# A three-mixer trunk on one core: sums of squares move from TensorE to VectorE, and the second layer's gates move into the first SSD turn

## The reference, cut to what matters

```
x = x + ab_mixer(rmsnorm(x))      # layer 0
x = x + c_mixer(rmsnorm(x))       # layer 1
y = rmsnorm(x)

_rms(x) = x * rsqrt(mean(x*x) + 1e-6)

# ab_mixer: 4 GLA heads and 4 mLSTM heads, each 512 wide
proj = h @ w_in_ab                # 2048 -> some 14,000 columns
o = recurrence(q, k, v, gates, state)            # per head
o = _rms(o) * norm_weight * silu(z)              # per head
y = o @ w_out_ab

# c_mixer: 64 SSD heads in 8 groups
z, xbc, dt = split(h @ w_in_c)
dt = softplus(dt + dt_bias); a = -exp(a_log)
xbc = silu(causal_conv4(xbc, conv_state))
y = ssd(xbc, dt, a, state)                       # decays exp(cumsum(dt*a))
y = _rms per group of (y * silu(z)); y = y @ w_out_c
```

## Time and profile before

| | |
|---|---|
| time, median of 3 runs | 2212.8 us (2210.91 to 2214.97) |
| the profiled execution: time, span | 2215.32 us, 2213.8 us |
| TensorE busy | 2108.5 us, 95% of the span |
| VectorE, ScalarE, GpSimd busy | 64%, 45%, 13% |
| DMA | 436.97 MB, mean 197 GB/s |
| granted TensorE clock, mean | 0.977 |

### The profile page before, as it was taken

The page is one execution under the profiler, slowest core; times in us unless marked ns, Lnnn a source line. Parts: engine busy times, 40 slices in busy tenths (PEclk is TensorE's granted clock), DMA queues, the critical chain, the costliest instruction groups (busy, mean ns, idle before and its releaser), DMA issues. The chain is left out here.

```text
span 2213.8 us, 41516 instructions
## 1 busy us (share of the span) xinstructions
PE 2108.5 (95%) x15171; PEld 1970.3 (89%) x15171; DVE 1416.6 (64%) x2602; ACT 1005.3 (45%) x1516; POOL 279.6 (13%) x423
## 2 busy tenths in 40 slices
PE   6999999999999999999999599999999999989997
PEld 4898989998989998998999599988989889879996
DVE  5553747566558475575644467887788788775544
ACT  3444444434433443343333346556466565564432
POOL 1010202010101011020100101121220211200000
PEclk8899999999999999999999799999999999999998
DMA  4484759485847568495965375665665765756851
GB/s 131 129 270 125 268 156 305 149 284 163 269 123 249 191 191 258 134 323 169 322 221 165 90 206 177 179 206 178 199 209 163 214 187 178 217 195 190 289 158 67
DMA packets 337191, 436.97 MB, mean 197 GB/s; under 512 B 17688, under 2 KB 296776, under 8 KB 335628
## 3 DMA queue, kind: packets, MB, share of 16 engines
q1 hardware_dynamic: 298476, 297.76, 44.3%
q0 software_dynamic: 38384, 137.67, 18.5%
q10 hardware_dynamic: 224, 0.05, 0.0%
HBM read 355.35 MB, written 80.06 MB: 197 GB/s over the span
## 5 line engine op out<-in xcount | busy, mean ns | idle before, releaser
L145 PE MATMUL bank<-xn_hi,w_hi 128*128 128x288 f32 x3584 | 1082.8, 302 | 26.3 <-issue 9.4
L146 PE MATMUL bank<-xn_lo,w_hi 128*128 128x288 f32 x3584 | 1063.6, 297 | 0.0
L147 PE MATMUL bank<-xn_hi,w_lo 128*128 128x288 f32 x3584 | 1061.1, 296 | 0.0
L132 DVE TENSOR_TENSOR w_lo<-w_raw,w_hi 128x1024 fp32r<-128x1024 f32 x512 | 624.5, 1224 | 628.3 <-ACT w_hi L126 618.8
L126 ACT ACTIVATE w_hi<-w_raw 128x1024 fp32r<-128x1024 f32 x512 | 541.2, 1060 | 947.8 <-PE bank L147 858.5
L145 PEld LDWEIGHTS bank<-xn_hi,w_hi 128*128 128x128 f32 x3584 | 679.2, 189 | 54.0 <-issue 39.5
L146 PEld LDWEIGHTS bank<-xn_lo,w_hi 128*128 128x128 f32 x3584 | 680.3, 190 | 5.6
L147 PEld LDWEIGHTS bank<-xn_hi,w_lo 128*128 128x128 f32 x3584 | 680.7, 190 | 0.0
L1258 DVE SCALAR_TENSOR_TENSOR state<-state,decay,bank 128x512 f32<-128x512 f32 x128 | 92.3, 742 | 0.0
L1865 POOL DMA_DIRECT2D out_ssm_s<-ssd_state x64 | 47.9, 756 | 307.7 <-DVE ssd_state L2293 244.3
L2132 ACT ACTIVATE ssd_state<-ssd_state,ssd_we 128x128 f32<-128x128 f32 x256 | 82.5, 414 | 0.0
(11 more groups left out here) (445 smaller groups left out, 2338.5 us busy)
## 6 DMA issues: line engine op xcount, KB each, us to landing
w_raw<-in_w_in_ab SPq DMA_DIRECT2D x224, 512.0 KB, 4.0
w_raw<-in_w_in_c SPq DMA_DIRECT2D x128, 512.0 KB, 4.1
w_raw<-in_w_out_ab SPq DMA_DIRECT2D x64, 512.0 KB, 4.8
w_raw<-in_w_out_c SPq DMA_DIRECT2D x64, 512.0 KB, 3.8
state<-in_state_gla POOLq DMA_DIRECT2D x32, 512.0 KB, 10.1
out_gla_s<-state POOLq DMA_DIRECT2D x32, 512.0 KB, 4.2
state<-in_state_mlstm_c POOLq DMA_DIRECT2D x32, 512.0 KB, 10.2
out_mc_s<-state POOLq DMA_DIRECT2D x32, 512.0 KB, 5.4
```

What stands on the lines that cost most here:

```text
L132: dve.tensor_tensor(core.w_lo[:, j], core.w_raw[:, j % RAW], core.w_hi[:, j].bitcast(F32), ALU.subtract).then_inc(ws["split"], 1)
L145: pe.matmul(banks[m][:, 0:T], core.w_hi[:, j, kk, col], hi[:, k], start=f, stop=False)
L146: pe.matmul(banks[m][:, 0:T], core.w_hi[:, j, kk, col], lo[:, k], start=False, stop=False)
L147: ins = pe.matmul(banks[m][:, 0:T], core.w_lo[:, j, kk, col], hi[:, k], start=False, stop=e)
```

## The change

1. **The three norms of the trunk** (setup and both rests): in place of sixteen ones products (`tensor_sum`, `t_sums`), VectorE copies the first squared tile to a buffer and adds fifteen (`vector_sum`), and TensorE runs one ones product over the sum (`tensor_total`). The rest's gate product goes to bank 4.
2. **AB heads:** VectorE adds four squared tiles in two instructions, and `t_rms` has one ones product.
3. **Gates:** the block `gates1` becomes the class `Gates1`, whose parts are placed in the first SSD turn: SP's loads ahead of the first group's, VectorE's parts at the turn's start and at steps 1, 2, 3, 4 and 6, ScalarE's at steps 0 and 2, TensorE's transposes at steps 3 and 5. POOL stores the tables (SP did) and waits for them and for the last copy before its loads of the group. The buffers lie over those of the mixer that are not yet used.

```diff
+    def vector_sum(self, dve, k, slot):
+        dve.wait_ge(self.squared, k + 1)
+        if isinstance(k, int) and k == 0:
+            dve.tensor_copy(self.tmp[:], self.sq[:, slot]).then_inc(self.sq_free, 1)
+        else:
+            dve.wait_ge(self.sq_free, k)
+            dve.tensor_tensor(self.tmp[:], self.tmp[:], self.sq[:, slot], ALU.add).then_inc(self.sq_free, 1)
+    def tensor_total(self, pe, bank):
+        pe.wait_ge(self.sq_free, KT)
+        pe.matmul(bank[:, 0:T], self.core.ones[:], self.tmp[:], start=True, stop=True).then_inc(self.total, 1)
...
                 dve.tensor_copy(xT[:, k], core.bank[k % 4][:, 0:T]).then_inc(norm.ready, 1)
+                if k >= 2:
+                    norm.vector_sum(dve, k - 2, (k - 2) % 4)
...
-                if k >= 3:
-                    norm.tensor_sum(pe, core.bank[4], k - 3)
-            for k in range(KT - 3, KT):
-                norm.tensor_sum(pe, core.bank[4], k)
+            norm.tensor_total(pe, core.bank[4])
...
-            pe.wait_ge(s["o_sq"], H + 1)
-            for f in range(4):
-                i = pe.matmul(B[6][:, 0:T], core.ones[:], sq[:, f], start=f == 0, stop=f == 3)
-            i.then_inc(s["rms"], 1)
+            pe.wait_ge(s["sq_sum"], H + 1)
+            pe.matmul(B[6][:, 0:T], core.ones[:], sq[:, 0], start=True, stop=True).then_inc(s["rms"], 1)
...
             if slot == 3:
+                dve.wait_ge(s["o_sq"], H + 1)
+                st.then_wait(dve.tensor_tensor(sq[:, 0:2], sq[:, 0:2], sq[:, 2:4], ALU.add))
+                dve.tensor_tensor(sq[:, 0], sq[:, 0], sq[:, 1], ALU.add).then_inc(s["sq_sum"], 1)
                 dve.wait_ge(s["rms"], H + 1)
...
             self.t_group(pe, pr * 2, 0)
-            self.t_sums(pe, (2, 3), pr * 4 - 2)
             self.t_group(pe, pr * 2 + 1, 1)
-            self.t_sums(pe, (0, 1), pr * 4)
-        self.t_sums(pe, (2, 3), KT - 2)
+        norm.tensor_total(pe, B[4])
...
                 self.v_group(dve, pr * 2 + par, par)
+                self.v_sums(dve, pr * 4 + (2 * par - 2), 2 - 2 * par)
         for og in (OG - 2, OG - 1):
...
             self.v_group(dve, og, og % 2)
+            self.v_sums(dve, 2 * og - 2, 2 - 2 * (og % 2))
+        self.v_sums(dve, KT - 2, 2)
...
+    def gpsimd(self, pool):
+        pool.wait_ge(self.nc_d, 1)
+        pool.dma_start(self.scr["negc"], self.au[:]).then_inc(self.saved, 16)
+        pool.wait_ge(self.pad_d, 1)
+        pool.dma_start(self.scr["we"], self.we[:]).then_inc(self.saved, 16)
+        pool.wait_ge(self.saved, 32)
+        pool.wait_ge(self.done, 1)
...
+    def tensor(self, pe, k):
+        core, B = self.core, self.core.bank
+        if k == 3:
+            pe.wait_ge(self.r_in, 16)
             for t in range(CT):
...
+        if k == 5:
+            pe.wait_ge(self.pad_d, 1)
+            pe.wait_ge(self.hist, 1)
             for n in range(K_N):
...
+        if k == 4:
+            dve.wait_ge(self.turned, 1)
             for i in range(3):
+                ins = dve.tensor_copy(g["hist"][:, 16 * i:16 * i + 16].rearrange("p t c -> p (t c)"), B[5 + i][:, 0:384])
+            ins.then_inc(self.hist, 1)
...
         @block.sync
         def _(sp):
+            g1.sync(sp)
             load_group(sp, 0)
...
         def _(pool):
+            g1.gpsimd(pool)
             load_nb(pool, 0)
             load_we(pool, 0)
             load_state(pool, 0, 0)
...
             with nc.cleanup_on_exit():
-                gates1(nc, core, io, scr, g)
-            with nc.cleanup_on_exit():
                 ssd_mixer(nc, core, io, out, scr, g, ws)
```

More of the change, by code:

```diff
@@ L191, in __init__ @@
         self.sq, self.var, self.r, self.tmp = sq, var, r, tmp
-        self.ready, self.squared, self.scaled, self.high, self.var_ok, self.r0, self.done, self.sq_free = (
-            sem(f"{tag}_{n}") for n in "x_ready squared scaled high variance r_first normed sq_free".split())
+        self.ready, self.squared, self.scaled, self.high, self.var_ok, self.r0, self.done, self.sq_free, self.total = (
+            sem(f"{tag}_{n}") for n in "x_ready squared scaled high variance r_first normed sq_free total".split())
         self.stored = [sem(f"{tag}_x_stored{q}") for q in range(KT // 4)]
@@ L1470, in gpsimd @@
             pool.wait_ge(self.gw_in, 16)
[L1472 to L1478, removed]
     def t_group(self, pe, og, par):
@@ L1566, in v_group, with v_sums @@
             dve.tensor_tensor(x, op.pairs[(par + op.par0) % 2][m][:, 0:T], x, ALU.add).then_inc(norm.ready, 1)
+    def v_sums(self, dve, n, slot):
+        for i in range(2):
+            self.norm.vector_sum(dve, n + i, slot + i)
     def vector(self, dve):
@@ L1609, in layer1_buffers @@
     return dict(hist=core.sb("ssd_history", [P, CT, 24], F32, ctx), cols=core.sb("ssd_cols", [P, K_N, SSD_H], F32, ctx))
[L1612 to L1654, removed]
@@ new lines, with __init__, sync, scalar @@
+class Gates1:
+    def __init__(self, core, sem, io, scr, g, ctx, gap):
+        self.core, self.io, self.scr, self.g = core, io, scr, g
+        sb = lambda n, s, d=F32: core.sb("g1_" + n, s, d, ctx)
+        self.crow, self.par = sb("conv_rows", [24, 6144]), sb("params", [64, 8])
+        self.dt, self.au, self.c, self.keep2, self.wx = (sb(n, [64, T]) for n in "dt au c keep wexp".split())
+        self.we, self.tot = sb("we", [64, 2 * TS]), sb("total", [64, 8])
+        sb("gap", [P, (gap - 4 * (6144 + 16 + 5 * T + 2 * TS)) // 4])
+        self.pad = sb("pad", [64, K_N * P])
+        (self.s_in, self.r_in, self.u_d, self.sp_d, self.wx_d, self.wx_e, self.pad_d, self.turned, self.nc_d, self.saved, self.hist,
+         self.done) = (sem("g1_" + n) for n in
+                       "small_in rows_in u softplus w_arg w_exp pad turned negc saved hist done".split())
+    def sync(self, sp):
+        io = self.io
+        sp.dma_start(self.par[:, 0:1], io["ssd_dt_bias"].rearrange("o h -> h o")).then_inc(self.s_in, 16)
+        sp.dma_start(self.par[:, 1:2], io["ssd_a_log"].rearrange("o h -> h o")).then_inc(self.s_in, 16)
+        sp.dma_start(self.crow[:], io["state_ssm_conv"][0].rearrange("b t c -> (b t) c")).then_inc(self.r_in, 16)
+    def gpsimd(self, pool):
[5 more added lines that the diff above has]
+        pool.wait_ge(self.done, 1)
+    def scalar(self, act, k, st):
+        if k == 0:
+            act.wait_ge(self.s_in, 32)
+            act.activation(self.par[:, 1:2], self.par[:, 1:2], ACT.Exp)
+            act.wait_ge(self.u_d, 1)
+            st.then_wait(act.activation(self.au[:], self.dt[:], ACT.Abs))
+            st.then_wait(act.activation(self.au[:], self.au[:], ACT.Exp, scale=-1.0))
+            act.activation(self.au[:], self.au[:], ACT.Ln, bias=1.0).then_inc(self.sp_d, 1)
+        if k == 2:
+            act.wait_ge(self.wx_d, 1)
+            act.activation(self.wx[:], self.wx[:], ACT.Exp)
+            act.activation(self.we[:, TS:2 * TS], self.we[:, TS:2 * TS], ACT.Exp).then_inc(self.wx_e, 1)
+    def tensor(self, pe, k):
+        core, B = self.core, self.core.bank
+        if k == 3:
+            pe.wait_ge(self.r_in, 16)
@@ L1660, in _, with vector @@
             for n in range(K_N):
-                i = pe.transpose(core.bank[1 + n // 8][:, 64 * (n % 8):64 * (n % 8) + 64], pad[:, n * P:(n + 1) * P],
+                i = pe.transpose(B[5 + n // 8][:, 64 * (n % 8):64 * (n % 8) + 64], self.pad[:, n * P:(n + 1) * P],
                                  core.ident[0:64, 0:64])
[L1663 to L1667, removed]
+            i.then_inc(self.turned, 1)
+    def vector(self, dve, k, st):
+        core, g, B = self.core, self.g, self.core.bank
+        par, dt, au, c, keep2, wx = self.par, self.dt, self.au, self.c, self.keep2, self.wx
+        pad, we, tot = self.pad, self.we, self.tot
+        cs = samples(c[:, S0:T])
+        if k is None:
@@ L1748, in ssd_mixer @@
         tmp.close()
+        with ExitStack() as over:
+            g1 = Gates1(core, sem, io, scr, g, over, ahead)
         op = OutProj(core, sem, io, scr, ws, True, 1)
@@ L2392, in _ @@
                     continue
+                if G is None:
+                    g1.vector(dve, None, st)
                 for i in range(SL):
```

66 lines of the change are left out of this document (37 added, 29 removed).

## The result

The changed kernel takes 2192.9 us (median of four runs, 2190.93 to 2193.48) against 2211.86 of the kernel before; the ratio is 0.9925, with a 95% interval of 0.9911 to 0.994. It is faster, by 19 us where 34.5 were forecast, and lies 4 us above the range. The profiled execution has a span of 2192.0 against 2213.8, 21.8 less; the profiled execution before was the slowest of its runs, so the trace shows some 3 us more than the medians do.

What follows compares the result with a forecast made beforehand. TensorE, busy 95% of the span, was taken as the bound. Setup −6.7, AB heads −5.8, output projections −9.9 and gates −12.1 sum to −34.5 us, giving 2180.8 profiled and 2178 median, range 2167 to 2189.

Steps and rivals of the forecast that it cites:

- Part A: Setup: VectorE's adds replace TensorE's ones products, and VectorE then sets a faster pace for the input tiles: −6.7 us.
- Part B: AB heads: six TensorE passes less, 1.44 us a head, counted for four of eight heads: −5.8 us.
- Part C: Two output projections: ones products leave TensorE's stream, −11.5 us for both, less .4 and 1.2 at the tails: −9.9 us.
- Part D: Gates between the layers: the 16.0 us block goes, and the first SSD turn takes part of it back: −12.1 us.
- the wait at step 5: First SSD turn: TensorE waits for history copies queued on VectorE behind a weight split: +1.5 us, bounds .5 and 4.
- Moved some 25 us later, it meets a ring that is full: -.8.: First SSD turn: GpSimd's 3.4 MB load of decay rows and states, moved later, no longer causes a .83 us stall.
- The granted clock ... I take 0.: First SSD turn: a start at the high clock level may give −2.1 us, a fall at a wait +2.1: 0.
- Rival 2: First SSD turn: waits at steps 3 and 5 for late VectorE (+4), two clock falls (+4.2): 2186 us; chance .17.
- The sign that the prediction had named for being wrong: First SSD turn longer by 8 us or more, with a granted clock below 1.
- Rivals 1: GLA heads gain as well, −5.8 us more: 2172.5 us; chance .10.
- 3: Setup is held by something else, late input tiles or the squares, and its gain is worth 1: 2184 us; chance .06.
- 4: Clock stays at the low level through the whole first SSD turn, +48 us: 2226 us, slower; chance .03.

Runs made afterwards that it cites:

- code moved by 32: The changed kernel with 32 idle semaphore instructions added to TensorE's program in the setup, so its later code lies 32 instructions further on: 2182.95 us, ratio 0.9883.
- shift by 256: The changed kernel with 256 idle semaphore instructions added to TensorE's program in the setup: 2217.97 us, ratio 1.0043.
- late states: The changed kernel with the first group's two halves of states loaded only behind units 13 and 17 of the first SSD turn: 2185.64 us, ratio 0.989.

## Why the prediction was wrong

**Part A** was right in its mechanism; it gave 7.5, not 6.7. That difference and the 1.6 behind the mixer's start cannot be told from spread: with the gates moved alone, whose setup is that of the kernel before, the mixer starts at 54.17 and not at 56.75, and the changed kernel's variants take 160.4 to 164.9 from there to the first ones product.

**Part B**: the price was right and the step to the whole was wrong. Each mLSTM head is 1.46 shorter at its ones product (forecast 1.44), and the GLA period is unchanged (100.51 after, 100.55 before). The code moved by 32 shows the whole term: from the first ones product to the projection's first matmul 880.61 against 888.13, -7.5. The sentence that failed is "six passes are 1.44 a head", taken as all that the edit does. In its place the heads gave .3 where 5.8 were forecast, since fewer instructions also move all code behind them: the stop hangs on where the code lies, as the runs with 32 and 256 show, and it fits them that the mLSTM loop's top came to lie just ahead of the edge of a 16 KB block. The Trainium skill (Runtime: NRT & Kernel Launch, Instruction fetch mechanics) says that code is loaded in blocks of 16 KB, 256 instructions, ahead of its use, and that a taken branch to code that is not loaded breaks this. The shift by 256, which restored the stop, agrees. No row of the kernel before shows the stop, since that kernel has none.

**Part C** was right: 5.72 and 6.09 a stream (forecast 5.75), tails .82 and 1.73 (.4 and 1.2).

**Part D**: the block's 16.0 were right (15.95), and the wait at step 5 and the transposes were within their bounds (.80, forecast 1.5; 3.5 for 48 and .8 for 10, forecast 3.2 with 6.4 as the bound). Two steps failed.
- "Moved some 25 us later, it meets a ring that is full: -.8." At the turn's start the burst had cost TensorE .83 us, with little but splits in ScalarE's and VectorE's queues. In the middle of the turn the convolution's tail and `xbc` stand behind the splits. I had looked for what needs the weights, and not for what is queued behind their split. Taking the burst apart gave 4.5 to 6.8.
- "The granted clock ... I take 0." The warm start was worth 2.0 as forecast, but the transposes cost a fall: 5.86 us for a unit of 3.2, and spread out they gave 3.2. A fall behind the 48 belonged into the sum, and not only into a rival; the 10 behind step 5 (.8 us) cost none, the unit behind them took 3.3.

Rival 2, with .17, had the size of it (8 us given back; 7.8 measured), but by the wrong wait: VectorE was late at units 14 and 19, not at steps 3 and 5. The sign that the prediction had named for being wrong did come: the first turn is 11.1 us longer than before (79.25 against 68.11), at a granted clock below 1. Rivals 1, 3 and 4 did not come. With the three causes mended the change gives 2175.07, against the 2178 forecast; that the two are close does not bear out each term, for the heads then gave 7.5 where 5.8 were forecast, and the first two SSD turns took back 1.7 where 3.9 were.

**Open**: the 1.78 at the end. From the output's transposes to the end are 17.4 to 17.5 us in the kernel before, in its two variants, and in the three changed kernels with 32 idle instructions, and 18.7 to 19.3 in the four with none or with 256. The traces divide in the same way: in those four one 16 KB instruction load falls into this stretch, in the other six none, and the 64 KB store that SyncE issues next to it takes 1.1 to 2.0 us to issue where such stores take .33 to .45 elsewhere. In the changed kernel, and with the code moved by 32:

```profile
2179.57 2.01 SPq L1462 DMA_DIRECT2D out_y_s<-oc_rows  x1
```

```profile
2170.55 0.44 SPq L1465 DMA_DIRECT2D out_y_s<-oc_rows  x1
```

So it too goes with where the code lies, but that is a correlation; no run took it apart. Nor was the transposes' fall tried without the late states.

## What to carry to other kernels

An edit that removes instructions moves all code behind it: if a stretch that the edit doesn't touch gets slower, look for idle time that no engine explains just behind a loop's top, and shift the code by a few instructions to test it. When a burst of transfers moves, ask not who needs the delayed data but what stands in order behind their first use on each engine. Put transposes between matmuls in small portions, and count a fall of the clock for a long stretch of them (here 2.7 us behind 3.5 us).

## What the runs showed of the hardware

- A stop for code of 2.2 to 2.8 us stands at the mLSTM loop's top in the four changed kernels with no shift or one of 256 instructions, and not with a shift of 32. With the low clock behind it, it costs a turn of the changed kernel 3.3 to 4.1 us.
- An idle semaphore instruction on TensorE takes about .15 us.
- In the loop of the GLA heads one 16 KB instruction load was seen in 213 us (242 to 455), in the mLSTM heads 26 in 384 us (646 to 1030): the loop with the longer turn (130 to 135 us, against 100.5) loads its code anew in each turn, the other does not.
